# Forty-two gathered tokens instead of thirty-two in a two-block decoder kernel with a dense expert pass

## The reference

```python
def peer(x, w_q, sub_keys, expert_u, expert_v):
    q = (x @ w_q).reshape(B, S, PEER_HEADS, 2, PEER_HALF)
    s = jnp.einsum('bshpk,hpnk->bshpn', q, sub_keys)
    top_s, top_i = lax.top_k(s, PEER_TOPK)            # 16 of 128 for each half
    ...                                               # 16 best of the 256 sums; ids = 128 i + j
    g = jax.nn.softmax(best_s, axis=-1)
    def block(args):
        xt, it, gt = args
        u = jnp.take(expert_u, it, axis=0)
        act = jax.nn.gelu(jnp.einsum('td,tkd->tk', xt, u)) * gt
        v = jnp.take(expert_v, it, axis=0)
        return jnp.einsum('tk,tkd->td', act, v)
```

## Time and profile before

| | |
|---|---|
| three runs | 2955.79, 2960.62, 2963.03 us (median 2960.62) |
| profiled execution, its own time | 2955.81 us |
| its span, first to last instruction | 2954.5 us |
| TensorE matmul busy | 2911.7 us, 99% |
| TensorE weight load busy | 2631.0 us, 89% |
| VectorE (DVE) busy | 2139.5 us, 72% |
| ScalarE (ACT) busy | 1570.7 us, 53% |
| GpSimd (POOL) busy | 419.0 us, 14% |
| memory read | 623 MB, 212 GB/s over the span |

### The profile page before, as it was taken

One profiled execution on the slowest core, in us unless ns is written; L12 is line 12 of the kernel. 1 busy time (PEld: TensorE's weight loads), 2 busy tenths in 40 slices (PEclk: granted clock), 3 DMA queues, 4 the chain that ended last, 5 costly groups with the idle time before them and its releaser, 6 DMA issues.

```text
span 2954.5 us, 45739 instructions
## 1 busy us (share of the span) xinstructions
PE 2911.7 (99%) x18502; PEld 2631.0 (89%) x18502; DVE 2139.5 (72%) x3352; ACT 1570.7 (53%) x2406; POOL 419.0 (14%) x304
## 2 busy tenths in 40 slices
PE   9999999999999999999998999999999999999998
PEld 7888888888888888899898999999999999999997
DVE  5566566666666455676589889778999777999776
ACT  4467755555555443577444556444556444556534
POOL 0011101111111000143020000232010133110131
PEclk9999999999999999999999999999999999999999
DMA  7544445555556554654564555788666788666784
GB/s 259 177 151 152 156 177 186 185 186 187 185 186 222 190 198 143 221 177 170 208 211 171 190 183 203 270 302 298 230 236 227 247 306 302 234 232 239 272 310 168
DMA packets 99009, 631.53 MB, mean 214 GB/s; under 512 B 11376, under 2 KB 12784, under 8 KB 31216
## 3 DMA queue, kind: packets, MB, share of 16 engines
q1 hardware_dynamic: 80368, 561.49, 54.3%
q0 software_dynamic: 18432, 67.12, 6.3%
HBM read 623.32 MB, written 4.19 MB: 212 GB/s over the span
## 4 chain that ended last, share of the span: by engine, by line
PE 78%; DMA 9%; DVE 8%; ACT 3%; issue 2%; SPq 0%; ACTq 0%; DVEq 0%
PE ps L292 26%; PE ps L293 13%; PE ps L1406 6%; PE ps L314 6%; PE ps L316 6%; PE ps L315 6%; DMA ring<-in_u_rows_dram,idx 5%; DMA ring<-in_v_rows_dram,idx 4%; PE ps L1408 3%; DVE loR L274 3%; PE ps L305 2%; PE ps L304 2%; PE ps L303 2%; ACT hiR L266 1%; PE ps L1311 1%
## 5 line engine op out<-in xcount | busy, mean ns | idle before, releaser
L274 DVE TENSOR_TENSOR loR<-raw,hiR 128x1024 fp32r<-128x1024 f32 x1017 | 1255.0, 1241 | 621.9 <-ACT hiR L266 618.4
L266 ACT CAST hiR<-raw 128x1024 fp32r<-128x1024 f32 x1026 | 1074.4, 1051 | 803.3 <-PE ps L1408 324.3
L292 PE MATMUL ps<-XA,hiR 128*128 128x448 f32 (+1 forms) x3936 | 1343.9, 391 | 10.7 <-DVE loR L274 9.3
L293 PE MATMUL ps<-XA,loR 128*128 128x224 f32 (+1 forms) x3936 | 1069.3, 272 | 0.0
L292 PEld LDWEIGHTS ps<-XA,hiR 128*128 128x128 f32 x3936 | 739.7, 188 | 127.1 <-DVE loR L274 6.6
L293 PEld LDWEIGHTS ps<-XA,loR 128*128 128x128 f32 x3936 | 747.7, 190 | 0.6
L1406 PE MATMUL ps<-hl,hiR 128*128 128x448 f32 x2048 | 651.0, 377 | 6.2 <-DVE loR L274 5.9
L1408 PE MATMUL ps<-hl,loR 128*128 128x224 f32 x2048 | 543.5, 265 | 0.0
L1406 PEld LDWEIGHTS ps<-hl,hiR 128*128 128x128 f32 x2048 | 385.2, 188 | 42.8 <-DVE loR L274 9.2
L1408 PEld LDWEIGHTS ps<-hl,loR 128*128 128x128 f32 x2048 | 392.1, 191 | 0.2 <-issue 0.2
L1447 POOL DMA_INDIRECT ring<-in_u_rows_dram,idx x64 | 103.2, 1612 | 716.8 <-DVE ring L1469 664.8
(11 more groups left out here) (307 smaller groups left out, 3490.1 us busy)
## 6 DMA issues: line engine op xcount, KB each, us to landing
raw<-in_u_dram SPq DMA_DIRECT2D x128, 1024.0 KB
raw<-in_v_dram SPq DMA_DIRECT2D x128, 1024.0 KB
raw<-in_w_up_dram SPq DMA_DIRECT2D x86, 1024.0 KB
raw<-in_w_down_dram SPq DMA_DIRECT2D x43, 1024.0 KB
raw<-in_w_in_qk_dram SPq DMA_DIRECT2D x32, 1024.0 KB
raw<-in_w_out_dram SPq DMA_DIRECT2D x32, 1024.0 KB
raw<-in_w_in_dram SPq DMA_DIRECT2D x24, 1024.0 KB
raw<-in_w_in_v_dram SPq DMA_DIRECT2D x16, 1024.0 KB
```

The lines of the kernel that those rows point to most:

```text
L266: e.copy(hiR[:, r:r + 2, :], raw[n % NR][:, q:q + 2, :]).then_inc(S("hi"), 1)
L274: e.tensor_tensor(loR[:, r:r + 2, :], raw[n % NR][:, q:q + 2, :], hiR[:, r:r + 2, :].bitcast(F32), ALU.subtract).then_inc(S("lo_pool" if p ...
L292: e.matmul(both, wh, X.hl[:, :, k, 0:nt], start=(k == 0), stop=False, skip_group_check=True)
L293: m = e.matmul(dst[:, 0:nt], wl, X.h[:, k, 0:nt], start=False, stop=(k == KC - 1), skip_group_check=True)
```

## The change

- TS is 42: 42 tokens are gathered, TD = 214 are dense. The gathered tokens stand in three groups of 42 partitions (126 in use, `GP`), so each partition has 43 experts (`ROWS`) and there are 172 gathers and row instructions instead of 128. The last group has one expert too many, with gate zero.
- `ring` has RN = 3 slots. A gather for slot m + 3 waits for use m.
- `PLACES`: 11 rows in U0 (from piece 70, every 9), 22 and 21 in U1 and U2 (every 7.3), and 42, 42 and 35 in V0, V1 and V2, every 3.9 to 4.0 pieces from piece 3 on, so also during f = 0.
- OJ is made by POOL: four `tensor_scalar` instructions of 128x128 for a group (`pool_gates`), with the second half key in float32 (`jf`). PE waits for them by a semaphore of their own. NG is 54.
- The index and gate data are written for all 128 partitions by 8 DVE instructions (`ixs`, `gss`), and six small DMAs on SP's queue move them to `idx` and `gs` (behind the fetch of the 13th tile of U0).
- `dve_rows_sum` works on all 128 partitions, `sel4` is zero outside the groups; some semaphores are shared and tiles are moved in memory. The rest of the diff (not shown) renames them.

```diff
@@ -13,7 +13,7 @@
 D = 2048
 T = 256
 
-TS = 32
+TS = 42
 TD = T - TS
...
-NR, NQ, LA = 3, 8, 4
+NR, NQ, LA, RN = 3, 8, 4, 3
 RANGES = [(0, 43), (43, 86), (86, 128)]
 NI = 43
 MIX = [c for h in range(8) for c in (h, 8 + h)]
@@ -83,10 +83,13 @@
 
 
 
-ROWS = 128 * TS // 128
+GROUPS = 128 // TS
+GP = GROUPS * TS
+ROWS = -(-128 // GROUPS)
 NROW = 2 * ROWS
-PLACES = [P_U[r] + 4 + 10 * k for r in (1, 2) for k in range((16, 15)[r - 1])]
-PLACES += [P_VV[r] + NI + 3 + int(3.5 * k) for r in range(3) for k in range((36, 36, 26)[r])]
+PLACES = [P_U[0] + 70 + 9 * k for k in range(11)]
+PLACES += [P_U[r] + 4 + int(7.3 * k) for r in (1, 2) for k in range((22, 21)[r - 1])]
+PLACES += [P_VV[r] + (3, 3, 3)[r] + int((3.9, 4.0, 3.9)[r] * k) for r in range(3) for k in range((42, 42, 35)[r])]
 SLOT = {p - P_U[0]: k for k, p in enumerate(sorted(PLACES))}
 assert len(SLOT) == 2 * NROW + 1
...
-    gated = at("gated", 15.625, [128, ROWS])
+    hrep, vsum = at("hrep", o + HV, [128, D]), at("vsum", o + HV, [128, D])
+    yT = [at("yT0", 8, [128, 8, TD]), at("yT1", o + HV + 8, [128, 8, TD])]
+    idx = at("idx", 14.75, [128, ROWS, 2], U32)
+    gs = at("gs", 15.125, [128, ROWS])
+    dots = at("dots", 15.3125, [128, ROWS, 2])
+    gated = at("gated", 15.6875, [128, ROWS])
+    ring = [at(f"ring{i}", (0, 4, o + HV + 14.75)[i], [128, 1024]) for i in range(RN)]
+    ixs = at("ixs", o + HV + 14.75, [128, GROUPS * ROWS, 2], U32)
+    gss = at("gss", o + HV + 16, [128, GROUPS * ROWS])
     o = RB + SG
     qT = [at(f"qT{i}", o - 16 + i, [128, T]) for i in range(16)]
     g5 = at("g5", o, [128, D])
...
@@ -1122,9 +1131,9 @@
                 e.activation(fl[6][:, :], fl[6][:, :], ACT.Exp).then_inc(S("d_exp"), 1)
             elif d == 14:
                 e.wait_ge(S("d_tr"), n + 1)
-                for i in range(2):
-                    e.copy(selb[:, i, half(tb)], bank[4][:, i * 128:(i + 1) * 128]).then_inc(S("sel_g"), 1)
-                e.mul(selb[:, 2, half(tb)], bank[4][:, 256:384], 4096.0).then_inc(S("sel_g"), 1)
+                e.copy(selb[:, 0, half(tb)], bank[4][:, 0:128]).then_inc(S("sel_g"), 1)
+                e.copy(jf[:, half(tb)], bank[4][:, 128:256]).then_inc(S("sel_g"), 1)
+                e.mul(selb[:, 1, half(tb)], bank[4][:, 256:384], 4096.0).then_inc(S("sel_g"), 1)
 
     def dve_choice(e, s):
         lo8, hi8 = slice(0, 8), slice(8, 16)
...
@@ -1245,27 +1254,27 @@
                 e.wait_ge(S("dec"), ND * n + 27)
                 e.tensor_tensor(v2(g_), v2(e1), rc.unsqueeze(2).to_broadcast([128, 8, 16]), ALU.mult).then_inc(S("dec"), 1)
             elif d == 10 and n == 0:
-                own, ids = slice(TD - 128, 128), xi
+                ids = xi
                 e.wait_ge(S("dec"), ND)
-                e.scalar_tensor_tensor(ids[own, :], I_[own, :], 128.0, J_[own, :], ALU.mult, ALU.add).then_inc(
-                    S("sp_ix"), 1)
+                e.scalar_tensor_tensor(ids[:, :], I_[:, :], 128.0, J_[:, :], ALU.mult, ALU.add).then_inc(S("sp_ix"), 1)
                 e.wait_ge(S("sp_ix"), 1)
-                e.tensor_scalar(ids[own, :], ids[own, :], 2.0, None, ALU.mult).then_inc(S("sp_ix"), 1)
+                e.tensor_scalar(ids[:, :], ids[:, :], 2.0, None, ALU.mult).then_inc(S("sp_ix"), 1)
                 e.wait_ge(S("sp_ix"), 2)
-                for j in range(128 // TS):
-                    part, cs = slice(TS * j, TS * j + TS), slice(ROWS * j, ROWS * j + ROWS)
-                    e.tensor_copy(idx[part, :, 0], ids[own, cs]).then_inc(S("sp_ix"), 1)
-                    e.tensor_scalar(idx[part, :, 1], ids[own, cs], 1.0, None, ALU.add).then_inc(S("sp_ix"), 1)
-                    e.tensor_copy(gs[part, :], g_[own, cs]).then_inc(S("sp_ix"), 1)
+                e.tensor_copy(ixs[:, 0:128, 0], ids[:, :]).then_inc(S("sp_ix"), 1)
+                e.tensor_copy(ixs[:, 128:129, 0], ids[:, 127:128]).then_inc(S("sp_ix"), 1)
+                e.tensor_scalar(ixs[:, 0:128, 1], ids[:, :], 1.0, None, ALU.add).then_inc(S("sp_ix"), 1)
+                e.tensor_scalar(ixs[:, 128:129, 1], ids[:, 127:128], 1.0, None, ALU.add).then_inc(S("sp_ix"), 1)
+                e.tensor_copy(gss[:, 0:128], g_[:, :]).then_inc(S("sp_ix"), 1)
+                e.memset(gss[:, 128:129], 0.0).then_inc(S("sp_ix"), 1)
             elif d == 14:
                 e.wait_ge(S("sel_g"), 3 * n + 3)
-                e.scalar_tensor_tensor(selb[:, 3, half(tb)], bank[4][:, 256:384], 4096.0, selb[:, 2, half(tb)],
+                e.scalar_tensor_tensor(selb[:, 2, half(tb)], bank[4][:, 256:384], 4096.0, selb[:, 1, half(tb)],
                                        ALU.mult, ALU.subtract).then_inc(S("sel"), 1)
 
 
     GATE0 = [DEC0 + 2 * DECP + 2 - 4 * 16, 1, 1]
     GATE_STEP = [2.0, 2.8, 2.7]
-    NG = TD // 4
+    NG = -(-TD // 4)
 
     def gate_at(r, s):
 
@@ -1282,31 +1291,36 @@
                 e.wait_ge(S("choice_const"), 48)
             if k >= 2:
                 e.wait_ge(S("g_mm"), k - 1)
-            if r == 0:
-                e.tensor_tensor(OJ[v][:, :].rearrange("p (a t) -> p a t", t=4),
-                                selb[:, 1:2, ts].to_broadcast([128, 128, 4]), ioh4[:, :, :], ALU.is_equal).then_inc(
-                    S("g_og"), 1)
-            else:
-                e.tensor_tensor(OJ[v][:, :].rearrange("p (t a) -> p t a", t=4),
-                                selb[:, 1, ts].unsqueeze(2).to_broadcast([128, 4, 128]),
-                                ioh4[:, :, 0].unsqueeze(1).to_broadcast([128, 4, 128]), ALU.is_equal).then_inc(
-                    S("g_og"), 1)
             e.tensor_tensor(OI[v][:, :, 0:ni], selb[:, 0, ts].unsqueeze(2).to_broadcast([128, 4, ni]),
                             ioh4[:, i0:i1, 0].unsqueeze(1).to_broadcast([128, 4, ni]), ALU.is_equal).then_inc(S("g_oi"), 1)
             e.wait_ge(S("g_oi"), k + 1)
             e.tensor_tensor(OG[v][:, :, :, 0:ni], OI[v][:, None, :, 0:ni].to_broadcast([128, 2, 4, ni]),
-                            selb[:, 2:4, ts].unsqueeze(3).to_broadcast([128, 2, 4, ni]), ALU.mult).then_inc(
+                            selb[:, 1:3, ts].unsqueeze(3).to_broadcast([128, 2, 4, ni]), ALU.mult).then_inc(
                 S("g_og"), 1)
+
+    def pool_gates(e, r, s):
+        for n in gate_at(r, s + 1):
+            k, v = NG * r + n, n % 2
+            if k == 0:
+                e.wait_ge(S("sel"), 2)
+                e.wait_ge(S("choice_const"), 48)
+            if k >= 2:
+                e.wait_ge(S("g_mm"), k - 1)
+            for j in range(4):
+                m = e.tensor_scalar(OJ[v][:, 128 * j:128 * j + 128], ioh4[:, :, 0], jf[:, 4 * n + j:4 * n + j + 1], None,
+                                    ALU.is_equal)
+            m.then_inc(S("g_oj"), 1)
 
     def pe_gates(e, r, s):
         ni = RANGES[r][1] - RANGES[r][0]
         for n in gate_at(r, s - 2):
             k, v, b = NG * r + n, n % 2, u_bank(r) + 2 + n % 2
-            e.wait_ge(S("g_og"), 2 * k + 2)
+            e.wait_ge(S("g_oj"), k + 1)
+            e.wait_ge(S("g_og"), k + 1)
             if n >= 2:
                 e.wait_ge(S("g_ev"), k - 1)
             for j in range(4):
-                of = slice(j, 512, 4) if r == 0 else slice(128 * j, 128 * j + 128)
+                of = slice(128 * j, 128 * j + 128)
                 for w in range(2):
                     m = e.matmul(bank[b][:, ni * j:ni * j + ni], OJ[v][:, of], OG[v][:, w, j, 0:ni], start=(w == 0),
                                  stop=(w == 1))
@@ -1317,7 +1331,8 @@
         for n in gate_at(r, s - 3):
             k, b = NG * r + n, u_bank(r) + 2 + n % 2
             e.wait_ge(S("g_mm"), k + 1)
-            e.mul(G_[:, 0:ni, 4 * n:4 * n + 4], bank[b][:, 0:4 * ni].rearrange("p (t i) -> p i t", t=4),
+            w = min(4, TD - 4 * n)
+            e.mul(G_[:, 0:ni, 4 * n:4 * n + w], bank[b][:, 0:w * ni].rearrange("p (t i) -> p i t", t=w),
                   1.0 / 4096).then_inc(S("g_ev"), 1)
 
 
...
@@ -1437,47 +1452,46 @@
         m = row_of(s - 1)
         todo = []
         if s == min(SLOT) - 14:
-            e.wait_ge(S("sp_ix"), 2 + 3 * (128 // TS))
-            e.wait_ge(S("x_out"), 16)
-            todo = [0, 1]
-        elif m is not None and m + 2 < 2 * NROW:
+            e.wait_ge(S("sp_load"), 32 * GROUPS)
+            todo = list(range(RN))
+        elif m is not None and m + RN < 2 * NROW:
             e.wait_ge(S("sp_use"), m + 1)
-            todo = [m + 2]
+            todo = [m + RN]
         for m in todo:
-            e.indirect_dma_start(ring[m % 2][:, :], None, A["u_rows" if m < NROW else "v_rows"],
-                                 bass.IndirectOffsetOnAxis(ap=idx[:, m % NROW // 2, m % 2:m % 2 + 1], axis=0)).then_inc(
-                S(f"row{m % 2}"), 16)
+            e.indirect_dma_start(ring[m % RN][0:GP, :], None, A["u_rows" if m < NROW else "v_rows"],
+                                 bass.IndirectOffsetOnAxis(ap=idx[0:GP, m % NROW // 2, m % 2:m % 2 + 1],
```

(38 more changed lines are left out.)

52 lines of the change are left out of this document (24 added, 28 removed).

## The result

The changed kernel takes 3115.73 us (median of five runs, 3106.91 to 3120.09), the kernel before, run beside it, 2955.79 (2952.80 to 2963.03). The ratio is 1.0529 with an interval of 1.0506 to 1.0553: 160 us slower. The forecast was 2914, in a range of 2897 to 2940, so sign and size are both wrong.

The account below looks back on a forecast made before the run. PE's own pace was taken to bound the kernel, with DVE next. The terms -50.6 - 2.1 - 10 + 10 + 4 + 1.5 + 1 make -46.2, so 2955.8 becomes 2909.6 profiled and 2914 us for the median, range 2897 to 2940.

Parts of the forecast that it names:

- Fewer columns: Matmul pairs: 30 columns less at 0.412 ns each take 12.4 ns off each of 4096 pairs, -50.6 us.
- low matmul doesn't shrink: Rival, matmul pairs: a floor under 224 columns leaves only 20 columns a pair, 34 us gained, 2931; chance 0.06.
- Gate groups: Gate matmuls on PE: 3 x 2 fewer groups at 0.36 us each, -2.1 us.
- choice: Choice of experts, where PE waits for DVE: column gain of 2.1 us lost, index writing about 0.6 less, +1.5 us.
- Ring of three: V passes: a third row slot removes nearly all of DVE's waits for gathered rows, -10 us, between 0 and -14.
- Rows in f = 0: V passes' f = 0: added rows overload DVE, costing 6 us in all, plus 4 in V2; +10, ends 0 and +25.
- One-hot rows on POOL: U passes: POOL instructions of 320 ns, 0.6 us with waits, nearly keep PE's group period; +4 us, ends 0 and +28.
- slower: Rival, U passes: POOL alternates with DVE, each instruction behind a whole split, 1.0 us each, about 3092; chance 0.05.
- It fits: DVE in U0: 26.6 us are free for 216 POOL instructions, 0.12 each, against 0.09 of port contention.
- Transfers: Rival, DMA: 327 GB/s wanted; if 313 is all, three long stretches each last some 7 us longer, 2935; chance 0.07.
- At no cost: Small DMAs, POOL's queue order, `dve_rows_sum` and merged semaphores: nothing, save +1 us taken in case the DMAs delay a tile.
- the signs that were to show it wrong: PE waiting on OJ over 10 us, U splits far above 1.3, a pair above 0.305, ACT tile waits over 20.

Follow-up runs that it names:

- both causes undone: Changed kernel with OJ made by DVE again and gathers over all 128 partitions, the rest of the change kept: 2925.96 us, ratio 0.9898 to the kernel before.
- the run with 32 columns: Changed kernel with each of POOL's one-hot instructions making 32 columns instead of 128, same count of instructions: 2999.45 us, one execution.
- the run that only writes: Changed kernel with POOL writing a constant by memset over 128 columns, four a group, instead of comparing: 2965.41 us, one execution.

## Why the prediction was wrong, step by step

Excess below is the time of a pass over its number of pairs times the pair's undisturbed pace, summed over the pairs that took longer.

- **What bounds the kernel.** Right: PE's pace. Undisturbed U and V pairs took 313.8 and 315.5 ns before and take 306.3 and 308.2 now (eight pairs for U, medians of stretches without a wait for V).
- **Fewer columns, -50.6: the mechanism was right, the term mis-sized.** Measured: 7.5 and 7.3 ns a pair times 2048 each, **-30 us**. The step of this term that failed is the slope: "I take the slope, since 224 and 256 lie close to 214." Between 256 and 224 both matmuls of a pair gain; from 224 down only the high one does, 20 columns for 7.5 ns. The rival *low matmul doesn't shrink* (34 us in place of 50.6) had this, at a chance of 0.06.
- **Gate groups, -2.1, and choice, +1.5.** With both causes undone the U passes lose 18.7 us, 15.4 of it by columns. The rest, 3.3, holds these two terms and was not taken apart.
- **Ring of three, -10.** Excess in V0 and V1 before is 3.6 and 6.1 us; in the kernel with both causes undone it is 0 in both after f = 0. So **-9.7**, the forecast's size, though not all by the third slot: that is worth 4 (two slots, 2930.0). The rest came with the other edits, the wider places among them, and was not taken apart.
- **Rows in f = 0, +10.** The mechanism was right, the size 16 in place of 10. Excess in f = 0 of V0, V1 and V2 is 3.0, 3.1 and 10.2 us, where 2, 2 and 6 were forecast, with DVE at 55.3 of 56.1 us. For V2 the cause given, end data ahead of the tiles, isn't it: there POOL's issue of one gather takes 16.16 us.
- **One-hot rows on POOL, +4 with ends 0 and +28: measured +127 to +137** against the same rows on DVE. This is the step that decided the sign, and two numbers in it failed. *Alone:* 320 ns were taken, "half the slope", between 183 and 461; it takes 595, above the upper end. The slope of 2.17 ns from two-input f32 rows was halved for having one input, when one input in f16 costs 2.55. *The wait:* 0.27 was taken, 0.357 measured. Even with the wait as forecast, 0.595 + 0.27 = 0.865 lies above the 0.80 at which the prediction had the gain gone. The upper bound was none: it took the price of a two-input row for the most that one input could cost, and no row said so. The check is the run with 32 columns: at 350 ns alone, close to the 320 taken, the cost is 20 us against rows on DVE, inside the ends of 0 and 28. The term itself counts from a POOL that holds nobody up, which the run that only writes comes nearest to; against that one (2965) it is 34, and that of the full instruction 150. Each of the two runs is a single execution.
- **The rival "slower"** (POOL alternating, 1.0 us an instruction, 3092, a chance of 0.05) is nearest to what came. That POOL's period, not PE's, sets the U passes is right, and the mean of 0.95 us is near its 1.0. But the wait isn't the one that it names, each instruction behind a whole split: with 0.9 us of wait it leaves 0.1 for the instruction itself, which takes 0.595, and the median of 631 ns says that most hardly wait. So the nearness of 1.0 is luck, and that of 3092 to 3116 as well. It has 182 us in U passes where 134 came, nothing for the gathers (60), and 20 too much of a gain for the columns. The period of a group by the starts of the first and last groups' matmuls, in U0 after, in U1 after, and in U0 with both undone:

```profile
1637.86 0.29 PE L1325 MATMUL ps<-OG,OJ 128*128 128x43 f16 x5
...
1842.02 0.24 PE L1325 MATMUL ps<-OG,OJ 128*128 128x43 f16 x3 [0.55 <-POOL OJ L1310]
...
2105.60 0.28 PE L1325 MATMUL ps<-OG,OJ 128*128 128x43 f16 x5 [2.21 <-DVE OG L1297]
...
2344.61 0.25 PE L1325 MATMUL ps<-OG,OJ 128*128 128x43 f16 x3
```
```profile
1639.75 0.31 PE L1334 MATMUL ps<-OG,OJ 128*128 128x43 f16 x4
...
1789.01 0.28 PE L1334 MATMUL ps<-OG,OJ 128*128 128x43 f16 x3
```

  Over 53 periods these are 3.85, 4.51 and 2.82 us. POOL's groups in the same two passes say what sets them:

```profile
L1310 POOL TENSOR_SCALAR OJ<-ioh,jf 128x128 f16<-128x128 f16 x216 | 190.2, 895 | 79.3 <-DVE selb L1271 78.7
```
```profile
L1310 POOL TENSOR_SCALAR OJ<-ioh,jf 128x128 f16<-128x128 f16 x213 | 209.1, 996 | 6.0 <-PE ps L1325 5.0
L1461 POOL DMA_INDIRECT ring<-in_u_rows_dram,idx x22 | 31.8, 1443 | 9.5 <-DVE ring L1483 5.6 <-issue 3.9
```

  In U0 four times 0.895 are 3.58, and the gathers (11 later ones of some 1.4 us in 54 groups) 0.28: 3.86. In U1 four times 0.996 are 3.98 and the gathers 0.59: 4.57. POOL's busy time is the period, within 2.5%: between the matmuls shown it is busy for 200.9 of 204.1 us and for 233.1 of 239.0. U0 loses (3.85 - 2.82) x 53 = 55 us, which is its whole difference from the kernel with both undone (300.2 - 245.4). By that account the granted clock of 0.95 and 0.97 in these passes has no share of its own: PE waits for POOL either way. No run tried that apart.
- **"It fits": DVE's side.** This part held. A split in U1 takes 1256 ns on average and 1281 in U0 with POOL beside it, against 1222, and DVE is busy for less of U1 than before (199.3 us against 218.4). POOL is the one that waits. DVE's free time was worked out; the time POOL needs was not bounded well.
- **Transfers.** The rival was named for the bandwidth (chance 0.07, +21). That 327 GB/s are wanted was no obstacle: with 128 partitions 328 are moved, at 0.90, with no gap on PE. What did come, **+60 us** (50 in V passes, where excess falls from 71.2 to 21.7 us with 128 partitions, and 10 in U passes), was not in the sum: the prediction counted bytes (0.52 MB, 126 rows of 4 KB) and put the partition count of a gather at nothing, without a reason. What the runs show in its place is 4 KB packets of 228 ns instead of 181. Nothing in the trace before showed a gather over fewer than 128 partitions. The diff did show `[0:GP, :]`, and no bound was given for it.
- **At no cost** (six small DMAs, queue order, merged semaphores): with both causes undone nothing in the waits points to them; they were not tried alone.

Together: -30 for columns, -3 for groups and choice, -9.7 for row waits, +6 in f = 0 of V0 and V1, +9 in V2, make -28, the sum of the pass differences between the kernel before and the one with both undone (1376.1 and 1347.6), and -30 in time. On top of that come 190 us for the two causes: 160 slower.

The prediction failed by one of the two loads that it had named as its weakest, OJ on POOL, and by one that it had not priced, the gathers over 126 partitions. Of the signs that were to show it wrong, three came: PE waits 102.9 us for OJ, a pair takes 0.3063, ACT waits 306.6 us for tiles. The fourth, splits far above 1.3 us on average in U, did not, as DVE is not the one that pays.

## What to carry to other kernels

Before work is moved to an idle engine, its whole period there (instructions, waits for the shared port, other duties) is to be set against that of the consumer, with a price above the nearest rows too where the trace has neither the operation nor its data type. Before columns are cut from a pair of matmuls, measure each of the two by itself, since one may have reached its floor. Of the three partition counts tried here (128, 126 and 112) an indirect gather was best made over all 128, with idle ones fetching a row that nobody uses; other counts and kernels are not tried.

## What the runs showed of the hardware that was not expected

- A one-input compare on GpSimd, 128 partitions, f16, costs 268 ns and 2.55 ns a column (350 at 32 columns, 595 at 128, least values); a write of the same 128 columns 204. Beside DVE instructions that mostly have two SBUF inputs it takes 952 on average (median 631), the write 212.
- Gathers of 4 KB rows over 126 partitions instead of 128 add 39 us to a kernel with 128 gathers (2994.5 against 2956), over 112 partitions 16 us by the ratio (1.0053). Going back to 128 takes 62 us off the kernel with 172 gathers and three slots. The packets last longer (181, 212 and 220 ns for 4 KB with 128, 126 and 112); the 4-byte packets between them, 9 to 13 ns each, weigh nothing.
- GpSimd's issue of one gather takes 1.12 to 1.97 us in V0's f = 0, and 4.6 to 5.2 us several times in a row and once 16.16 us in V2's. The cause is open.
- A pair of matmuls at 448 columns high takes 313.8 ns with 224 or 214 low columns, and 317.5 with 160: fewer columns, more time.
